# A hybrid encoder layer on one core: where two additions, eight bank drains and the row factor are done

## The chip, the cores and the metric

The kernel runs on one core of a Trainium2 chip. The metric is device time in microseconds (us) of one execution, the median over several runs. TensorE (PE in the profile) does matrix products into PSUM; VectorE (DVE), ScalarE (ACT) and GpSimd (POOL) do elementwise work; SyncE (SP) issues the loads. Every engine works its own queue in order, and they meet only by semaphores.

## What is computed

One layer over 256 tokens of width 2048, batch 1, all in float32. The input is normalised by row, multiplied by `w_in`, and its columns go to three mixers (attention in a neighbourhood, an RWKV7 recurrence in both directions, retention); their outputs are concatenated and multiplied by `w_out`; a feed-forward part with `w_up` and `w_down` (8192 wide) follows. The parts that matter here:

```python
h = rms_norm(x, pre_mix_g[l]);  z = h @ w_in[l]          # row factor 1/rms, one for each token
# attention: softmax(q k^T * 64**-0.5 + bias) v, 8 heads of 64
# recurrence, end: y = layer_norm(y) * lnx_g + lnx_b ; y = y + bonus ; y_rw = y * g
# retention, 6 heads of 128:
q = rotary_interleaved(q, ang); k = rotary_interleaved(k, ang) * d ** -0.5
#   rotary: stack([x0 * cos - x1 * sin, x0 * sin + x1 * cos])
o = intra + cross; o = o * rsqrt(mean(o * o) + eps); yc = o * silu(g)
y = concatenate([ya, yb, yc]) @ w_out[l]
```

## The kernel before

**Weights.** All weight matrices stream through as halves of 128x1024 values. SP loads a half into `raw` (four slots). ScalarE rounds it to float32r, `hi` (L1614, `w_hi`), VectorE forms the rest, `lo` (L979, `w_lo`), three slots each. TensorE multiplies high by high, high by low and low by high (L2065, L2066, L2071 and others). This stream goes on for the whole kernel.

**Groups.** `w_in` gives 57 tiles of 128 columns, in 29 groups of two. The first 11 groups belong to the recurrence. Of the other 18, two tiles fill one PSUM bank (6 or 7 in turn) as 128x512. Groups 11 and 12 are the attention's queries, 13 and 14 its keys, 15 and 16 its values, 17 and 18 the first values of retention, 19 to 24 the pairs (query, key) of retention heads 0 to 5, 25 more values, 26 to 28 the gates. Values are drained by ScalarE with a factor per token (`by_token`). The other 13 groups are drained by VectorE: `scaled_nr` (L1016, its instruction L1023) multiplies the bank by `row_scale`, the row factor, on its way to SBUF, and raises `bank_free`. Draining group g waits for `bank_free` of the group before, and TensorE starts group g when g-2 is drained.

**Gaps.** The products of `w_in` are cut into "gaps" by a list of depths, `DONE`. Every engine has its own `gap()`, in which it does its share of what is due by then: drains of groups first, then `hi` or `lo`. Between gaps an engine does the mixers' work, written out by hand. `stage_a` runs the recurrence (six tiles, its last a tail of four chunks); the mix stage follows.

**Mix stage.** It has six turns, `turn(i)` on each engine, one for each retention head; the first four also carry two attention heads each. In turn i:
- GpSimd, ahead of it, turns head i by the table: L913 multiplies query and key by `cos` into `qk_cos`, L917 the key's halves by `sin` into `qk`. L917 waits for `st_done`, the retention scores of head i-1 (L2481 on TensorE).
- VectorE, in `rotate(i)`: L1394 multiplies the query's halves by `sin`, L1398 adds `qk_cos`. L1398 waits for `rot_in`, all four products of GpSimd.
- VectorE: `scale_q(i)` (L1353, four instructions, reading the query's tokens backwards, times 64**-0.5) feeds the attention scores; `maxima(i)` adds the bias (L1369) and takes negative maxima (L1374, L1377). ScalarE exponentiates (L1901, `weights`). VectorE divides by the sums (`scale_p`: L1403, L1405). TensorE transposes the result (`turn_p`, L2471), ScalarE copies it back (L1866).
- In turn 0 VectorE also does, behind `maxima(1)`, `summed_recurrence` (L1381, `y_rw` plus the bonus in `zr`, 128x1536) and `gated_recurrence` (L1386, times `gate`), which raises `y_rw_ready`. ScalarE waits for `y_rw_ready` before it writes `o_all` (L1933), which lies over `gate`.

GpSimd's work ahead of the mix stage is the attention bias: it waits for `table_in` (the table with `win`, `cos`, `sin`) and `bias_in`, and adds `win` to eight heads (L905).

## Time and profile before

| | |
|---|---|
| median of three runs | 1303.27 us (1302.81 to 1303.52) |
| the profiled execution | 1303.43 us, span in the trace 1301.6 us |
| granted TensorE clock, mean | 0.998 of full speed |
| busy: PE, DVE, ACT, POOL | 1284.9, 825.2, 644.9, 323.6 us |
| chain that ended last | PE 91%, DVE 4%, all others 1% or less |

The span is the time from the first to the last instruction in the trace; the profiled execution took 1.83 us more than it. Times within the trace, such as 434.92, count from the start of the span. An idle stretch of an engine stands in square brackets behind the instruction that ended it, with the releaser. Rows of one engine overlap by a few tens of ns where the next instruction is already under way.

### The profile page before, as it was taken

What the parts mean: (1) busy time and instruction counts of PE and PEld (TensorE: products, weight loads), DVE (VectorE), ACT (ScalarE), POOL (GpSimd) and SP (SyncE); (2) the same over time, 40 slices, a digit from 0 to 9 for tenths busy, and PEclk for the clock granted to TensorE, in tenths of its full rate; (3) what the DMA queues carried; (4) which work ended last, traced back from release to release, by engine and by line L of the source; (5) the groups of instructions that cost most, each with busy time, mean ns of one, the idle gap of its engine ahead of it and who ended that gap; (6) DMA issues with size and microseconds to landing.
All of it is one profiled execution on the core that took longest, in us unless ns stands there. A gap on an engine that the chain in (4) does not pass through costs nothing.

```text
span 1301.6 us, 24350 instructions
## 1 busy us (share of the span) xinstructions
PE 1284.9 (99%) x9986; PEld 1103.2 (85%) x9986; DVE 825.2 (63%) x1148; ACT 644.9 (50%) x985; POOL 323.6 (25%) x266
## 2 busy tenths in 40 slices
PE   9999999999999999999999999999999999999997
PEld 7888888778899898888888888888888888888886
DVE  7778887887767877556555555555555555555564
ACT  6565655555435565546444444444444444444453
POOL 0224332333214320002444445555510000000000
PEclk9999999999999999999999999999999999999999
DMA  9766333342385456745766666666655555555572
GB/s 302 196 180 191 100 87 108 88 115 82 113 187 162 116 154 224 259 146 150 224 194 186 188 192 189 186 192 190 189 191 194 192 193 194 194 194 193 194 239 86
DMA packets 267695, 226.24 MB, mean 174 GB/s; under 512 B 15232, under 2 KB 240640, under 8 KB 266944
## 3 DMA queue, kind: packets, MB, share of 16 engines
q1 hardware_dynamic: 267344, 223.51, 57.0%
q8 instruction: 79, 1.29, 0.4%
q0 software_dynamic: 240, 1.18, 0.3%
q14 instruction: 32, 0.26, 0.1%
HBM read 222.56 MB, written 2.10 MB: 173 GB/s over the span
## 4 chain that ended last, share of the span: by engine, by line
PE 91%; DVE 4%; SPq 1%; DMA 1%; issue 1%; ACT 1%; DVEq 0%; ACTq 0%
PE psum L2535 33%; PE psum L2081 23%; PE psum L2092 12%; PE psum L2065 3%; PE psum L2071 3%; PE psum L2066 3%; PE psum L2145 2%; PE psum L2308 1%; DVE w_lo L979 1%; PE psum L2147 1%; PE psum L2152 1%; SPq L743 1%; PE psum L2243 1%; PE psum L2106 1%; PE psum L2323 1%
## 5 line engine op out<-in xcount | busy, mean ns | idle before, releaser
L979 DVE TENSOR_TENSOR w_lo<-raw,w_hi 128x1024 fp32r<-128x1024 f32 x393 | 500.9, 1277 | 373.8 <-ACT w_hi L1614 370.8
L1614 ACT ACTIVATE w_hi<-raw 128x1024 fp32r<-128x1024 f32 x393 | 417.7, 1064 | 440.6 <-PE psum L2535 196.9
L2535 PE MATMUL psum<-w_hi,act_both 128*128 128x512 f32 x1216 | 327.6, 389 | 0.1
L2081 PE MATMUL psum<-act_both,w_hi 128*128 128x512 f32 x1296 | 315.4, 392 | 0.0
L2081 PEld LDWEIGHTS psum<-act_both,w_hi 128*128 128x128 f32 x1296 | 237.0, 188 | 45.2 <-issue 0.2
L2535 PEld LDWEIGHTS psum<-w_hi,act_both 128*128 128x128 f32 x1216 | 228.0, 188 | 48.6 <-DVE arena L1555 0.5
L2535 PE MATMUL psum<-w_lo,act_both 128*128 128x512 f32 x608 | 187.5, 389 | 0.0
L2092 PEld LDWEIGHTS psum<-act_both,w_lo 128*128 128x128 f32 x1296 | 169.4, 191 | 7.7
L2092 PE MATMUL psum<-act_both,w_lo 128*128 128x256 f32 x1296 | 173.2, 283 | 0.0
L2535 PEld LDWEIGHTS psum<-w_lo,act_both 128*128 128x128 f32 x608 | 114.1, 188 | 23.6
L924 POOL TENSOR_TENSOR arena<-arena 128x512 f32<-128x512 f32 x32 | 42.3, 1323 | 285.8 <-DVE arena L1555 285.8
L2065 PE MATMUL psum<-act_both,w_hi 128*128 128x256 f32 x416 | 113.1, 304 | 0.0
L2066 PE MATMUL psum<-act_both,w_hi 128*128 128x256 f32 x416 | 104.2, 282 | 0.0
L2065 PEld LDWEIGHTS psum<-act_both,w_hi 128*128 128x128 f32 x416 | 78.8, 189 | 5.3 <-issue 1.2
L2066 PEld LDWEIGHTS psum<-act_both,w_hi 128*128 128x128 f32 x416 | 79.2, 190 | 0.2
L927 POOL TENSOR_SCALAR arena<-arena 128x512 f32<-128x512 f32 x32 | 74.1, 2314 | 2.8
L2071 PE MATMUL psum<-act_both,w_lo 128*128 128x256 f32 x416 | 68.8, 283 | 0.7 <-DVE w_lo L979 0.7
L929 POOL TENSOR_TENSOR arena<-arena 128x512 f32<-128x512 f32 x32 | 61.5, 1922 | 2.7
L2071 PEld LDWEIGHTS psum<-act_both,w_lo 128*128 128x128 f32 x416 | 58.0, 191 | 1.3 <-DVE w_lo L979 1.3
L2145 PE MATMUL psum<-w_hi,act_both 128*128 128x512 f32 (+1 forms) x96 | 37.2, 396 | 0.2 <-DVE arena L1023 0.2
L826 POOL TENSOR_TENSOR arena<-arena,row_scale 128x512 f32<-128x512 f32 (+1 forms) x11 | 18.1, 1649 | 68.6 <-DVE arena L1014 46.2
L2147 PE MATMUL psum<-w_hi,act_both 128*128 128x512 f32 (+1 forms) x96 | 33.4, 357 | 0.0
(251 smaller groups left out, 1238.0 us busy)
## 6 DMA issues: line engine op xcount, KB each, us to landing
raw<-in_w_up SPq DMA_DIRECT2D x128, 512.0 KB, 4.0
raw<-in_w_down SPq DMA_DIRECT2D x128, 512.0 KB, 4.4
raw<-in_w_in SPq DMA_DIRECT2D x113, 512.0 KB, 4.1
raw<-in_w_out SPq DMA_DIRECT2D x32, 512.0 KB, 4.7
arena<-in_na_rpb SPq DMA_DIRECT2D x16, 128.0 KB, 5.2
arena<-in_x SPq DMA_DIRECT2D x2, 1024.0 KB, 7.2
arena<-in_x_t SPq DMA_DIRECT2D x3, 512.0 KB, 7.7
out_x<-arena SPq DMA_DIRECT2D x3, 512.0 KB, 2.7
```

The lines of the kernel that those rows point to most:

```text
L927: pool.tensor_scalar(r, r, 0.0, None, ALU.max).then_inc(s["up_scaled"], 1)
L929: pool.tensor_tensor(u[:, 2 * q:2 * q + 2], r, r, ALU.mult).then_inc(s["relu_free"], 1)
L979: dve.tensor_tensor(by_half(h, low(h)), by_pair(h, raw[:, place[h] % RAW]), by_half(h, high(h)).bitcast(F32), ALU.subtract).then_inc(s["lo ...
L1614: act.activation(by_half(h, high(h)), by_pair(h, raw[:, place[h] % RAW]), ACT.Copy).then_inc(s["hi_half"], 1)
L2065: pe.matmul(dst, w_hi[:, h % SPLIT, at:at + P], act_hi[:, kt], start=kt == 0, stop=False)
L2066: pe.matmul(dst, w_hi[:, h % SPLIT, at:at + P], act_lo[:, kt], start=False, stop=False)
L2071: last = pe.matmul(dst, w_lo[:, h % SPLIT, at:at + P], act_hi[:, kt], start=False, stop=kt == KT - 1)
L2081: last = pe.matmul(bank[b], w_hi[:, h % SPLIT, at:at + P], act_both[:, kt].rearrange("p a t -> p (a t)"), start=kt == 0, stop=stop and kt ...
L2092: last = pe.matmul(bank[b][:, 0:T], w_lo[:, h % SPLIT, at:at + P], act_hi[:, kt], start=False, stop=stop and kt == kts[-1])
L2145: pe.matmul(dst, act_lo[:, kt, tokens], w, start=kt == 0 and (t == 0 or count == 4), stop=False, skip_group_check=count != 4)
L2147: pe.matmul(dst, act_hi[:, kt, tokens], w, start=False, stop=False, skip_group_check=count != 4)
L2535: last = pe.matmul(bank[4 * t + 2 * j + b], lhs[:, tokens], w[:, b * 512:(b + 1) * 512], start=start, stop=stop)
```

## The change

- `summed_recurrence` and `gated_recurrence` leave VectorE's turn 0. GpSimd does both, between its rotations of head 1 and of head 2, and waits for their end before it goes on.
- GpSimd multiplies `cos` and `sin` in the table by `row_scale` once (one 128x512 operation), ahead of the bias. VectorE's first rotation waits for that (`table_scaled`) in place of `table_in`.
- `scale_q` multiplies by 64**-0.5 and by `row_scale` in one instruction of the other form.
- With the factor in the table and in the queries, eight groups need none at the drain: 11 and 12 (attention queries) and 19 to 24 (retention queries and keys). ScalarE copies their banks (`copy_nr`) where VectorE multiplied them. Groups 13, 14, 26, 27 and 28 stay with VectorE.

```diff
+        def plain(g):
+            j = 2 * (g - RW_GROUPS)
+            return 0 <= j < NA_T // 3 or PLACE_OF[RET_Q(0)] <= j <= PLACE_OF[RET_K(RET_CT - 1)]
 # gpsimd
             pool.wait_ge(s["table_in"], 16)
+            angles = table[:, LATE["cos"][0]:LATE["sin"][1]].rearrange("p (a t) -> p a t", a=2)
+            pool.tensor_tensor(angles, angles, row_scale.unsqueeze(1).broadcast_to([P, 2, T]), ALU.mult).then_inc(
+                s["table_scaled"], 1)
+            pool.wait_ge(s["table_scaled"], 1)
...
+            def summed_recurrence():
+                pool.wait_ge(s["yt_taken"], RW_CT)
+                pool.tensor_tensor(y_rw, y_rw, zr, ALU.add).then_inc(s["y_rw_sum"], 1)
+            def gated_recurrence():
+                pool.wait_ge(s["y_rw_sum"], 1)
+                pool.wait_ge(s["gate_ready"], 3)
+                pool.tensor_tensor(y_rw, y_rw, gate, ALU.mult).then_inc(s["y_rw_ready"], 1)
...
+                if i == 1:
+                    pool.wait_ge(s["rot_in"], 4 * i + 4)
+                    summed_recurrence()
+                    gated_recurrence()
+                    pool.wait_ge(s["y_rw_ready"], 1)
 # vector
-                    if wide_of(at["nr"]) is None:
+                    if wide_of(at["nr"]) is None and not plain(at["nr"]):
                         scaled_nr(at["nr"])
...
-                    last = dve.tensor_scalar(q_s[:, h * GRID_W:(h + 1) * GRID_W], backwards(na_q(i), h * GRID_W),
-                                             NA_HD ** -0.5, None, ALU.mult)
+                    last = dve.scalar_tensor_tensor(q_s[:, h * GRID_W:(h + 1) * GRID_W], backwards(na_q(i), h * GRID_W),
+                                                    NA_HD ** -0.5, backwards(row_scale, h * GRID_W), ALU.mult, ALU.mult)
...
-                if i == 0:
-                    summed_recurrence()
-                    gated_recurrence()
 # scalar
+            def copy_nr(g):
+                tiles = group_tiles(g)
+                j = tiles[0] - RW_T
+                act.wait_ge(s["gemm_half"], 2 * (tiles[-1] + 1))
+                act.wait_ge(s["bank_free"], g)
+                place_free(act, j)
+                act.activation(cut(nr_at(j), 2 * T), bank[6 + g % 2], ACT.Copy).then_inc(s["bank_free"], 1)
...
                     if wide_of(at["wide"]) is not None:
                         by_token(at["wide"])
+                    elif plain(at["wide"]):
+                        copy_nr(at["wide"])
```

How the queues stand. Line numbers of the changed kernel differ; operands name the arrays they lie in, `arena` for nearly all.

GpSimd, from the bias to the rotation of head 2, before (L913 and L917 are a rotation):

```order
L905 TENSOR_TENSOR arena<-arena,arena_later 128x512 x8
L913 TENSOR_TENSOR arena_later<-arena,arena_later 128x256 x2
L917 TENSOR_TENSOR arena_later<-arena,arena_later 64x256 x2
L913 TENSOR_TENSOR arena_later<-arena,arena_later 128x256 x2
L917 TENSOR_TENSOR arena_later<-arena,arena_later 64x256 x2
L913 TENSOR_TENSOR arena_later<-arena,arena_later 128x256 x2
```

and changed (L931 and L935 are a rotation, L907 the table, L920 and L925 sum and gate):

```order
L907 TENSOR_TENSOR arena_later<-arena_later,row_scale 128x512
L914 TENSOR_TENSOR arena<-arena,arena_later 128x512 x8
L931 TENSOR_TENSOR arena_later<-arena,arena_later 128x256 x2
L935 TENSOR_TENSOR arena_later<-arena,arena_later 64x256 x2
L931 TENSOR_TENSOR arena_later<-arena,arena_later 128x256 x2
L935 TENSOR_TENSOR arena_later<-arena,arena_later 64x256 x2
L920 TENSOR_TENSOR arena_later<-arena_later,arena 128x1536
L925 TENSOR_TENSOR arena_later<-arena_later,arena 128x1536
L931 TENSOR_TENSOR arena_later<-arena,arena_later 128x256 x2
```

The table stands ahead of all of it, and two operations on 128x1536 between the second and the third rotation.

VectorE, from the end of `rotate(1)` in turn 0 to the first `scale_p` of turn 1, before:

```order
L1398 TENSOR_TENSOR arena_later<-arena_later 128x512
L1023 TENSOR_TENSOR arena<-psum,row_scale 128x512
L979 TENSOR_TENSOR w_lo<-raw,w_hi 128x1024
L1369 TENSOR_TENSOR arena_later<-psum,arena 128x1024
L1374 TENSOR_REDUCE small<-arena_later 128x4
L1377 TENSOR_SCALAR small<-small 128x4
L1381 TENSOR_TENSOR arena_later<-arena_later,arena 128x1536
L1386 TENSOR_TENSOR arena_later<-arena_later,arena 128x1536
L1403 RECIPROCAL small<-small 128x2
L1405 TENSOR_TENSOR arena_later<-arena_later,small 128x512
```

and changed:

```order
L1412 TENSOR_TENSOR arena_later<-arena_later 128x512
L1002 TENSOR_TENSOR w_lo<-raw,w_hi 128x1024
L1392 TENSOR_TENSOR arena_later<-psum,arena 128x1024
L1397 TENSOR_REDUCE small<-arena_later 128x4
L1400 TENSOR_SCALAR small<-small 128x4
L1417 RECIPROCAL small<-small 128x2
L1419 TENSOR_TENSOR arena_later<-arena_later,small 128x512
```

Three operations are gone between the rotation and `scale_p`: the drain of group 24, the sum and the gate.

ScalarE, in the recurrence's last chunk, where group 22 is due (L1843 and L1865 take a gate bank, L1817 and L1839 one product of the chunk, L1821 and L1843 of the changed kernel the next, L1614 and L1625 are `hi`), before:

```order
L1843 ACTIVATE arena<-psum 128x512
L1817 ACTIVATE arena<-psum 128x128
L1614 ACTIVATE w_hi<-raw 128x1024
L1821 ACTIVATE arena_later<-psum 64x2x64
L1614 ACTIVATE w_hi<-raw 128x1024 x3
```

and changed:

```order
L1865 ACTIVATE arena<-psum 128x512
L1839 ACTIVATE arena<-psum 128x128
L1668 ACTIVATE arena<-psum 128x512
L1625 ACTIVATE w_hi<-raw 128x1024
L1843 ACTIVATE arena_later<-psum 64x2x64
L1625 ACTIVATE w_hi<-raw 128x1024 x3
```

The copy stands right ahead of a `hi`; the seven others do too.

## Rows read from the trace of the kernel before

**Rows 1.** Page: the span, and the engines' busy time, share and instructions.

```profile
span 1301.6 us, 24350 instructions
...
PE 1284.9 (99%) x9986; PEld 1103.2 (85%) x9986; DVE 825.2 (63%) x1148; ACT 644.9 (50%) x985; POOL 323.6 (25%) x266
```

**Rows 2.** TensorE's waits: line, releaser, us in total, times, longest.

```profile
PE psum L2471 <- DVE arena_later L1405: 1.7, 1, 1.7
```

**Rows 3.** Timeline of VectorE, 422 to 435: start, length, line, operation, [idle before].

```profile
422.40 1.22 DVE L979 TENSOR_TENSOR w_lo<-raw,w_hi 128x1024 fp32r<-128x1024 f32 x1 [1.72 <-ACT w_hi L1614]
...
425.15 0.68 DVE L1023 TENSOR_TENSOR arena<-psum,row_scale 128x512 f32<-128x512 f32 x1
425.75 1.44 DVE L979 TENSOR_TENSOR w_lo<-raw,w_hi 128x1024 fp32r<-128x1024 f32 x1
...
429.60 0.17 DVE L1377 TENSOR_SCALAR small<-small 128x4 f32<-128x4 f32 x1
429.68 1.75 DVE L1381 TENSOR_TENSOR arena_later<-arena_later,arena 128x1536 f32<-128x1536 f32 x1
431.47 2.18 DVE L1386 TENSOR_TENSOR arena_later<-arena_later,arena 128x1536 f32<-128x1536 f32 x1
...
433.75 1.02 DVE L1405 TENSOR_TENSOR arena_later<-arena_later,small 128x512 f32<-128x512 f32 x1
```

**Rows 4.** Timeline of TensorE, at 434.9.

```profile
434.92 0.41 PE L2471 MATMUL psum<-cst,arena_later 128*128 128x128 f32 x2 [1.68 <-DVE arena_later L1405]
```

**Rows 5.** Timeline of ScalarE, at 422.9 and 429.8.

```profile
422.85 1.06 ACT L1614 ACTIVATE w_hi<-raw 128x1024 fp32r<-128x1024 f32 x1 [0.49 <-PE psum L2071]
429.81 0.51 ACT L1901 ACTIVATE arena_later<-arena_later,small 128x256 f32<-128x256 f32 x1 [5.89 <-DVE small L1377]
```

**Rows 6.** Timeline of GpSimd, 386 to 435.

```profile
386.45 11.94 POOL L905 TENSOR_TENSOR arena<-arena,arena_later 128x512 f32<-128x512 f32 x8 [3.82 <-DMA arena_later<-in_late]
...
411.31 1.44 POOL L913 TENSOR_TENSOR arena_later<-arena,arena_later 128x256 f32<-128x256 f32 x2 [8.00 <-DVE arena_later L1398]
414.61 1.88 POOL L917 TENSOR_TENSOR arena_later<-arena,arena_later 64x256 f32<-64x256 f32 x2 [1.86 <-PE psum L2481]
425.37 2.41 POOL L913 TENSOR_TENSOR arena_later<-arena,arena_later 128x256 f32<-128x256 f32 x2 [8.88 <-DVE arena_later L1398]
430.82 3.41 POOL L917 TENSOR_TENSOR arena_later<-arena,arena_later 64x256 f32<-64x256 f32 x2 [3.04 <-PE psum L2481]
```

**Rows 7.** Timeline of VectorE one turn later, 441 to 448.

```profile
441.73 0.85 DVE L1394 TENSOR_TENSOR arena_later<-arena,arena_later 64x256 f32<-64x256 f32 x2
...
445.74 0.17 DVE L1377 TENSOR_SCALAR small<-small 128x4 f32<-128x4 f32 x1
...
447.27 0.69 DVE L1405 TENSOR_TENSOR arena_later<-arena_later,small 128x512 f32<-128x512 f32 x1
```

**Rows 8.** Single lines: count, shortest/median/longest ns, first and last start.

```profile
L905 POOL TENSOR_TENSOR arena<-arena,arena_later x8: 1286/1302/2308, 386.4 to 396.1; 128x512 f32<-128x512 f32 x8
...
L913 POOL TENSOR_TENSOR arena_later<-arena,arena_later x12: 728/739/1724, 398.3 to 473.7; 128x256 f32<-128x256 f32 x12
...
L979 DVE TENSOR_TENSOR w_lo<-raw,w_hi x393: 1205/1226/2172, 10.2 to 1275.4; 128x1024 fp32r<-128x1024 f32 x197
...
L1353 DVE TENSOR_SCALAR arena_later<-arena x16: 177/181/725, 402.6 to 451.5; 128x64 f32<-128x64 f32 x16
```

**Rows 9.** ScalarE's groups by shape, 300 to 500: busy us, mean ns.

```profile
L1866 ACT ACTIVATE arena_later<-psum 128x512 f32<-128x512 f32 x8 | 4.8, 598 | 11.8 <-PE psum L2471 11.8
```

**Rows 10.** Timelines at 396: VectorE, then TensorE.

```profile
395.65 0.29 DVE L1279 COPY arena_later<-psum 64x128 f32<-64x128 f32 x1
...
396.09 0.30 PE L2413 MATMUL psum<-arena_later 128*64 128x64 f32 x3 [0.21 <-DVE arena_later L1279]
```

**Rows 11.** Timelines at 180: ScalarE, then TensorE.

```profile
179.76 0.29 ACT L1817 ACTIVATE arena<-psum 128x128 f32<-128x128 f32 x1
...
180.55 0.25 PE L2387 MATMUL psum<-arena 64*64 64x64 f32 x2
```

More of the change, by code:

```diff
@@ L436, in layer @@
         s = {n: sem(n) for n in (
-            "consts_in", "vec_in", "lora_in", "g2_in", "bias_in", "table_in", "decay_in", "gain_in", "x_again", "out_written",
+            "consts_in", "vec_in", "lora_in", "g2_in", "bias_in", "table_in", "table_scaled", "decay_in", "gain_in", "x_again", "out_written",
             "eps_set", "ones_set", "first_x_in", "first_raw_in", "first_hi", "first_lo", "x_squared", "x_added", "x_totalled", "x_summed", "row_root", "row_ready", "token_root", "token_ready", "token_done", "xt_done", "h_hi", "h_lo",
@@ L1377, in maxima @@
                 dve.tensor_scalar(top, top, -1.0, None, ALU.mult).then_inc(s["mx_ready"], 1)
-            def summed_recurrence():
-                dve.wait_ge(s["yt_taken"], RW_CT)
-                dve.tensor_tensor(y_rw, y_rw, zr, ALU.add).then_inc(s["y_rw_sum"], 1)
-            def gated_recurrence():
-                dve.wait_ge(s["y_rw_sum"], 1)
-                dve.wait_ge(s["gate_ready"], 3)
-                dve.tensor_tensor(y_rw, y_rw, gate, ALU.mult).then_inc(s["y_rw_ready"], 1)
             def rotate(i):
@@ L1390, in rotate @@
                 if i == 0:
-                    dve.wait_ge(s["table_in"], 16)
+                    dve.wait_ge(s["table_scaled"], 1)
                 dve.wait_ge(s["st_done"], i)
```

## The prediction

> **What bounds the kernel now.** I read the page first. TensorE is busy 1284.9 of 1301.6 us [rows 1], so the most that any change of the other engines can give back is what TensorE idles, 16.7 us, and the start and the end of the kernel hold a good part of that. A busy share of 63% on VectorE or 25% on GpSimd says nothing here. The second view is therefore TensorE's waits, one by one. Where a wait names an operation that the change touches, or one queued behind it, the change can pay. The longest of these is the transpose of the softmax in turn 1 (L2471), which waits 1.7 us for VectorE's L1405 [rows 2]. Then come the timelines around it.
>
> On TensorE the transpose starts at 434.92 after 1.68 us idle, so TensorE was ready at 433.24 [rows 4]. On VectorE the maxima end at 429.77 (429.60 + 0.17). Then the sum (429.68, 1.75 us) and the gate (431.47, 2.18 us) run to 433.65, and only then L1405, at 433.75 for 1.02 us, to 434.77 [rows 3]. ScalarE began the exponentials at 429.81 [rows 5], so they were not what was late. The 3.9 us of sum and gate stand in VectorE's queue in front of the one thing that TensorE wants.
>
> **Sum and gate leave VectorE.** What is late next? One turn later the same step has nothing between: from the end of the maxima (445.74 + 0.17 = 445.91) to the end of the first L1405 (447.27 + 0.69 = 447.96) it takes 2.05 us [rows 7]. In turn 1 the maxima also come 0.68 us earlier, since the drain of group 24 (425.15) leaves VectorE too [rows 3]: 429.77 - 0.68 = 429.09, and L1405 ends at 431.14. TensorE asks at 433.24. Cover 2.1 us, so the whole 1.68 us goes. Afterwards TensorE, VectorE and ScalarE are all 1.68 us earlier; their steps wait for each other and for TensorE, and the DMA has landed long before, so nothing takes it back that I can find.
>
> **The same two on GpSimd.** It can begin when the rotation of head 1 is done: L917 at 414.61 for 1.88, so 416.49 [rows 6]. The trace has no 128x1536 operation on GpSimd. Bounds: 128x512 takes 1.302 us and 128x256 takes 0.739 [rows 8], 0.563 us for 256 columns more, so 1536 columns take 1.302 + 4 x 0.563 = 3.55 us and both 7.1 us: done at 423.6. The upper bound is the worst stretch in the rows, 1724 against 728 ns for L913 [rows 8], 2.37 times: 16.8 us, done at 433.3. VectorE works half of this stretch on operands in SBUF, and a mixed stretch is L905's, eight in 11.94 us where 8 x 1.302 is 10.4 [rows 6, 8]; a bad one is the L917 pair at 430.82, 3.41 against 1.88 us [rows 6]. I take 1.4 times, 10 us: done at 426.5.
>
> Who waits? Queued behind them on GpSimd is the rotation of head 2. L913 began at 425.37 and took 2.41 us, then waited 3.04 us for TensorE's L2481, until 430.82 [rows 6]. At 426.5 it ends at 428.9, well ahead of that. Even from 433.3 the pairs of 2.41 and 3.41 us would end at 439.1, and VectorE's part of that rotation began at 441.73 [rows 7], now about 440.0. The other reader is ScalarE's `o_all`, held by `y_rw_ready`; that came at 433.65 before, and would now come at 426.5, at the worst bound at 433.3. Both are covered: price 0.
>
> The price on VectorE is contention. Gate against sum, same shape, is 2.18 against 1.75 us while L917 ran beside it [rows 3, 6]; L979 goes from 1.205 to 2.172 us at the worst [rows 8]. Behind 422.40, where VectorE still idles 1.72 us for ScalarE [rows 3], two L979 and a rotation can meet GpSimd's two operations: 0 to 2 x 0.97 + 0.5 = 2.4 us. Of the 2.1 us cover that leaves +2.1 to -0.3 us: at the worst 0.3 us of the wait stays. I take about 1 us of stretch and no price.
>
> The Trainium skill speaks against this part: GPSIMD Engine Reference, Key points, says that GpSimd shares its SBUF interfaces with VectorE, with contention from VectorE instructions that read two SBUF inputs, and that VectorE is about twice as fast at elementwise work. The trace agrees in direction (3.55 us worked out against 1.75 us measured). By that rule the two cost more engine time than they save; it would change the sum only if the cover of 2.1 us were used up.
>
> **The table by the row factor.** One more 128x512 operation on GpSimd at 386.45, 1.3 to 2.3 us by L905's range [rows 8]. It pushes the bias and the rotation of head 0 back by as much. After that rotation GpSimd idled 8.00 us for VectorE's L1398 [rows 6]: it was far ahead. Price 0; without that cover it would be 1.3 to 2.3 us.
>
> **The query scaling.** Sixteen L1353 of 0.181 us [rows 8] become the two-input form. Between no change and the length of one under contention, 0.725 us; near the lower end, since 64 columns are mostly fixed cost. I take +0.05 us each, 0.2 us a turn. In each turn VectorE next waits for a `hi`, or the scores it feeds are asked for later. Price 0.
>
> **Eight drains change engine.** VectorE gives back 8 x 0.68 us. ScalarE takes a plain PSUM copy of 128x512 each, 0.598 us (L1866) [rows 9], 4.8 us in all. Each stands right ahead of a `hi` that waits for the same progress of TensorE, so it never waits for more than that `hi` did; it delays it by 0.6 us. Two places matter.
> - Group 22, at 394. VectorE's L1279 began at 395.65, behind the drain, and TensorE waited 0.21 us for it until 396.09 [rows 10]. Without the drain L1279 comes 0.6 us earlier. ScalarE's half of the same value (L1821) comes 0.6 us later, behind its copy. Gain 0.2 us; 0 if L1821 is then late in turn.
> - Group 12, at 176. ScalarE's copy comes ahead of the L1817 that ended at 180.05, and TensorE used it at 180.55 [rows 11]. A slack of 0.5 us against 0.6 us: loss 0.1 us, at most 0.6.
>
> At group 24, `hi` ran at 422.85 [rows 5]; copied first it ends at 424.5, and VectorE wants it at 425.15. The other copies fall into idle time of ScalarE.
>
> **The sum.** -1.68 - 0.2 + 0.1 = -1.8 us. The profiled execution took 1303.43 us, 0.16 over the median 1303.27; the median becomes 1301.5 us, 0.14% less. A measurement of this kernel can tell about 0.2%, 2.6 us, from no change, so I call this "same".
>
> **Rivals.**
> - Contention eats the cover. L1405 in turn 1 is still late by up to 1.7 us, because both engines stretch each other (the rule of the skill, carried to its end). For it: 2.37 times for L913 and 1.8 times for L979. Against it: the cover of 2.1 us and the idle 1.72 us at 422.40. Time 1302 to 1303.3. Chance 0.12.
> - The 1.7 us is only moved: TensorE comes earlier to the next `lo` or `hi`, which was just in time, and waits there. For it: VectorE is busy nearly without a break in turns 0 to 3. Against it: those steps are themselves released by TensorE. Time about 1303. Chance 0.09.
> - More goes than I count: TensorE's short stalls for VectorE in the recurrence and the mix stage, too short to be listed or listed at well under 1 us, shrink as VectorE loses 8 x 0.68 + 3.9 = 9.3 us. Against it: only the drain at 394 stands ahead of such a wait. Some 2 us more, 1299.5 us. Chance 0.10.
> - Slower: `hi` is in fact what TensorE's next half hangs on, and the eight copies push it. 8 x 0.6 = 4.8 us, less 1.9: 1303.27 + 2.9 = 1306.2 us. It decides where the slack of a `hi` is under 0.6 us. Against it: in the whole list of TensorE's waits `w_hi` is named once, at the kernel's start. Chance 0.07.
>
> **How the numbers follow.** The forecast, 1300.8 to 1302.3, has 0.62. The two cases where the gain fails (0.21) end within 0.2% too. Faster by over 0.2%: 0.10. Slower: 0.07. Within: 0.83. The range reaches down towards the third rival and up over the first two, and leaves the slow one out: 1300.2 to 1303.6.
>
> **What would show it.** Right: no wait of TensorE before the transpose of turn 1, VectorE going from maxima straight to `scale_p`; sum and gate on GpSimd from about 415 to 427, 4 to 6 us each, with the rotation of head 2 behind them still waiting for TensorE; no wait before the state product at 396; copies on ScalarE of 0.6 us; TensorE's busy time unchanged. Wrong: a wait for L1405 or for a `lo` in turn 1 or 2; ScalarE's `o_all` waiting for GpSimd; TensorE waiting for `w_hi`; a new wait of over 0.3 us near group 12 or 19; a change of the span outside 390 to 440.

## The result, and the profile after

The changed kernel takes 1310.43 us (median of six, 1309.70 to 1311.43), the kernel before 1303.30 us beside it (median of six, 1302.81 to 1303.88). The ratio is 1.0055, with a 95% interval of 1.0045 to 1.0066: **slower by 7.1 us**, where 1301.5 us was predicted and 1303.6 us was the upper end.

The page has the span, and the engines' busy time, share and instructions, against [rows 1]:

```profile
span 1308.8 us, 24353 instructions
...
PE 1287.5 (98%) x9986; PEld 1104.9 (84%) x9986; DVE 825.5 (63%) x1138; ACT 648.1 (50%) x993; POOL 330.9 (25%) x269
```

TensorE has as many instructions as before and is busy 2.6 us more; VectorE has ten instructions fewer and is busy no less (825.5 against 825.2 us). Both are signs: something made the same work slower.

TensorE's waits come next (line, releaser, us in total, times, longest). The 1.7 us for the softmax scaling [rows 2] are gone, as forecast. In their place:

```profile
PE psum L2093 <- DVE w_lo L1002: 6.1, 3, 5.4
...
PE psum L2409 <- ACT arena L1839: 1.2, 1, 1.2
...
PE psum L2400 <- issue: 0.7, 1, 0.7
...
PE psum L2480 <- ACT arena_later L1878: 0.2, 1, 0.2
```

The first row's 5.4 us is one wait for a low half, `w_lo`, of which nothing in the change speaks. VectorE's timeline there (start, length, line, operation) says why it was late:

```profile
418.13 3.81 DVE L1419 TENSOR_TENSOR arena_later<-arena_later,small 128x512 f32<-128x512 f32 x1
421.86 4.43 DVE L1002 TENSOR_TENSOR w_lo<-raw,w_hi 128x1024 fp32r<-128x1024 f32 x1
...
427.43 1.21 DVE L1002 TENSOR_TENSOR w_lo<-raw,w_hi 128x1024 fp32r<-128x1024 f32 x1
```

L1419 is the scaling of the softmax, `scale_p`, of turn 0; it takes 3.81 us, where the same shape took 0.69 us [rows 7]. L1002 is the subtraction that makes the low half; it takes 4.43 us, against 1.2 us in the last row and in [rows 8]. Neither had to wait for a semaphore; the lost time is inside the instructions. GpSimd's timeline has what ran beside them, the table (L907), the rotation (L935, L931), the sum (L920) and the gate (L925):

```profile
388.70 1.27 POOL L907 TENSOR_TENSOR arena_later<-arena_later,row_scale 128x512 f32<-128x512 f32 x1 [5.40 <-DMA arena_later<-in_late]
...
415.93 1.54 POOL L935 TENSOR_TENSOR arena_later<-arena,arena_later 64x256 f32<-64x256 f32 x2 [1.20 <-PE psum L2503]
417.55 3.84 POOL L920 TENSOR_TENSOR arena_later<-arena_later,arena 128x1536 f32<-128x1536 f32 x1
421.47 3.75 POOL L925 TENSOR_TENSOR arena_later<-arena_later,arena 128x1536 f32<-128x1536 f32 x1
433.47 1.73 POOL L931 TENSOR_TENSOR arena_later<-arena,arena_later 128x256 f32<-128x256 f32 x1 [8.26 <-DVE arena_later L1412]
```

Put side by side, the ends answer each other. The sum ends at 421.39 (417.55 + 3.84), and the scaling that began at 418.13 ends at 421.94, 0.55 us later. The gate ends at 425.22, and the low half that began at 421.86 ends at 426.29, 1.07 us later. Each VectorE instruction did nearly all of its own work (0.69 and 1.22 us) after the GpSimd instruction had ended. By this it was not slowed down but **held**; the experiments below test that.

The trace of the kernel before has the same picture in small. Here is one of its two longest L979 [rows 8], with the GpSimd product beside it:

```profile
91.34 2.17 DVE L979 TENSOR_TENSOR w_lo<-raw,w_hi 128x1024 fp32r<-128x1024 f32 x1 [0.26 <-ACT w_hi L1614]
```

```profile
91.23 1.20 POOL L826 TENSOR_TENSOR arena<-arena,row_scale 128x512 f32<-128x512 f32 x1 [9.58 <-DVE arena L1014]
```

The product ends at 92.43 and L979 1.08 us later, at 93.51.

TensorE's timeline behind the wait (the low products, the transposes of the softmax, the scores of head pair 1):

```profile
426.35 1.65 PE L2093 MATMUL psum<-act_both,w_lo 128*128 128x256 f32 x6 [5.42 <-DVE w_lo L1002]
427.80 1.05 PE L2493 MATMUL psum<-cst,arena_later 128*128 128x128 f32 x4
428.79 2.08 PE L2480 MATMUL psum<-arena,arena_later 64*128 64x256 f32 x8
```

and the busy time of the engines and the granted TensorE clock in stretches of 5 us (the clock is the last but two):

```profile
415.00:420.00 5.00, 5.00 (x41) 4.89 (x41) 3.73 (x6) 3.95 (x11) 3.92 (x3) 1.00 0.04 13
420.00:425.00 5.00, 0.94 (x8) 0.73 (x7) 5.00 (x2) 0.73 (x1) 4.92 (x2) 0.89 0.00 0
425.00:430.00 5.00, 3.65 (x16) 3.15 (x18) 3.63 (x8) 1.10 (x2) 0.21 (x1) 0.50 0.42 110
430.00:435.00 5.00, 5.00 (x39) 3.69 (x36) 4.37 (x6) 1.98 (x3) 1.53 (x1) 0.92 0.71 203
```

Behind the wait the granted clock is 0.50 of full speed, the lower of the two levels, 1.2 instead of 2.4 GHz. Until 420 it stood at 1.00; then TensorE did nothing for 5.4 us. The six low products take 1.65 us.

One smaller loss stands earlier. ScalarE's timeline at 333 us, first after, then before (L1668 is the copy of group 19, L1625 and L1614 the high half behind it):

```profile
332.83 0.59 ACT L1668 ACTIVATE arena<-psum 128x512 f32<-128x512 f32 x1
333.45 1.14 ACT L1625 ACTIVATE w_hi<-raw 128x1024 fp32r<-128x1024 f32 x1
```

```profile
333.02 1.17 ACT L1614 ACTIVATE w_hi<-raw 128x1024 fp32r<-128x1024 f32 x1
```

and what TensorE does with it at 341 us, after and before:

```profile
341.19 0.45 PE L2400 MATMUL psum<-arena 64*64 64x64 f32 x8 [0.74 <-issue]
```

```profile
340.52 0.45 PE L2378 MATMUL psum<-arena 64*64 64x64 f32 x8 [0.20 <-issue]
```

The copy puts the high half 0.43 us later, the low half and the recurrence's chain on VectorE follow, and TensorE waits 0.74 instead of 0.20 us.

### The profile page after: what moved, and what is told of

Same layout as the page of the kernel before. It is cut to its first block, busy times and chain, and to the rows that moved or that the text cites. A ratio compares the mean times of both kernels' runs of the same rounds, so it can differ in the third digit from the quotient of the medians.

```text
span 1308.8 us, 24353 instructions
## 1 busy us (share of the span) xinstructions
PE 1287.5 (98%) x9986; PEld 1104.9 (84%) x9986; DVE 825.5 (63%) x1138; ACT 648.1 (50%) x993; POOL 330.9 (25%) x269
## 4 chain that ended last, share of the span: by engine, by line
PE 68%; DVE 3%; issue 1%; SPq 1%; ACT 1%; DMA 1%; DVEq 0%; POOL 0%; ACTq 0%
PE psum L2557 33%; PE psum L2103 18%; PE psum L2114 9%; PE psum L2087 1%; PE psum L2093 1%; PE psum L2088 1%; SPq L748 1%; DVE w_lo L1002 1%; DMA raw<-in_w_in 1%; PE psum L2534 0%; PE psum L2480 0%; PE psum L2167 0%; PE psum L2174 0%; PE psum L2169 0%; PE psum L2493 0%
## 5 line engine op out<-in xcount | busy, mean ns | idle before, releaser
L1002 DVE TENSOR_TENSOR w_lo<-raw,w_hi 128x1024 fp32r<-128x1024 f32 x393 | 505.5, 1288 | 378.2 <-ACT w_hi L1625 374.3
L1625 ACT ACTIVATE w_hi<-raw 128x1024 fp32r<-128x1024 f32 x393 | 417.7, 1064 | 439.1 <-PE psum L2557 195.7
```

What stands on the lines that cost most here:

```text
L1002: dve.tensor_tensor(by_half(h, low(h)), by_pair(h, raw[:, place[h] % RAW]), by_half(h, high(h)).bitcast(F32), ALU.subtract).then_inc(s["lo ...
L1625: act.activation(by_half(h, high(h)), by_pair(h, raw[:, place[h] % RAW]), ACT.Copy).then_inc(s["hi_half"], 1)
```

## The experiments

Two theories were to be told apart from the start. By the first, a VectorE instruction that meets a GpSimd instruction is held until that one ends, so the price goes by the length of one instruction. By the second, the two engines share a rate, so the price goes by the amount of work. Beside them stood two questions: what the clock costs, and what the other three parts of the change do. Every run has the time of the kernel before on the same chip beside it: 1302.71 us in the first series of four, 1302.69 in the second, 1302.61 in the third.

### The rest of the change alone

The changed kernel; the two calls leave GpSimd's loop and stand in VectorE's `turn` again:

```
-                if i == 1:
-                    pool.wait_ge(s["rot_in"], 4 * i + 4)
-                    summed_recurrence()
-                    gated_recurrence()
-                    pool.wait_ge(s["y_rw_ready"], 1)
...
                     maxima(i + 1)
+                if i == 0:
+                    summed_recurrence()
+                    gated_recurrence()
```

> The changed kernel with the sum and the gate back on VectorE, where they stood: the scaled angle table, the query scaling and the eight ScalarE copies alone. Theory (the long GpSimd instructions are what costs): the 5.4 us wait of the low products is not there, the 1.7 us wait for the softmax scaling is there again, the granted clock stays at 1.00 in 400 to 450 us, and the time is 1303.3 to 1304.6 us, the part above 1303.3 being the ScalarE copies' own price (the low halves ran 0.3 to 1.0 us late between 345 and 402 us in the changed kernel). Rival (the copies and the table carry a good part of the loss): 1306 us or more.

Measured: 1301.64 us, ratio 0.9993 (0.9984 to 1.0002), so 1.1 us under before, and below the range that I had set, though the interval takes in 1. The 5.4 us wait is gone and the clock stays at 1.00. TensorE's timeline shows the transposes of turn 1:

```profile
433.23 0.63 PE L2491 MATMUL psum<-cst,arena_later 128*128 128x128 f32 x4 [0.47 <-DVE arena_later L1414]
```

The wait there is 0.47 us, not the 1.68 of [rows 4]. I had expected it back in full. It is shorter because group 24's bank is no longer emptied by VectorE ahead of it, the 0.68 us that the prediction worked out; and the two operations took 1.75 and 1.76 us in this execution, against 1.75 and 2.18 [rows 3]. So the other parts do not carry the loss.

### The move alone

The kernel before, with the two operations defined and called on GpSimd, behind the rotation of head 1:

```
-                if i == 0:
-                    summed_recurrence()
-                    gated_recurrence()
...
+                if i == 1:
+                    pool.wait_ge(s["rot_in"], 4 * i + 4)
+                    summed_recurrence()
+                    gated_recurrence()
+                    pool.wait_ge(s["y_rw_ready"], 1)
```

> The kernel before with the sum and the gate moved to GpSimd and nothing else changed. Theory (the long GpSimd instructions are what costs): one VectorE instruction near 418 us takes some 3.8 us instead of 0.7 to 0.9 and the low half behind it some 4.4 instead of 1.2, TensorE waits 5 to 6 us for it, the clock falls behind it, and the time is 1308 to 1310 us. Rival (the parts only hurt together): under 1305 us.

Measured: 1308.33 us, ratio 1.0039 (1.0024 to 1.0054), 5.6 us over before. VectorE's timeline and TensorE's wait:

```profile
416.26 3.79 DVE L1410 TENSOR_TENSOR arena_later<-arena_later,small 128x512 f32<-128x512 f32 x1
419.98 4.43 DVE L993 TENSOR_TENSOR w_lo<-raw,w_hi 128x1024 fp32r<-128x1024 f32 x1
```

```profile
PE psum L2073 <- DVE w_lo L993: 6.1, 3, 5.4
```

The same two instructions are held for the same lengths, 3.79 and 4.43 us, and TensorE waits the same 5.4 us. The move does it by itself.

### The changed kernel once more

Unchanged, in the second series, since the two runs above add up to 4.5 us and not to 7.1.

> The changed kernel once more, unchanged, beside the others of this series. The move alone cost 5.6 us and the rest alone gained 1.1 us, 4.5 us together, where the whole change lost 7.1 us. If the parts hinder each other (the copies make the low halves late, and the long GpSimd instructions then hit a VectorE without slack), this run is again 6.5 to 7.5 us above before. If 7.1 us was partly a matter of when transfers landed in those executions (a raw half landed 1.3 us later at 393 us in its trace), it is 4 to 6 us above before, and the 2.3 us that stood between the two traces at 415 us are not there.

Measured: 1309.00 us, ratio 1.0051 (1.0035 to 1.0066), 6.3 us over before: between the two cases that I had set, within reach of both. Its waits:

```profile
PE psum L2093 <- DVE w_lo L1002: 6.1, 3, 5.4
...
PE psum L2400 <- issue: 0.8, 1, 0.8
```

The 1.2 us of L2409 above, at 395 us (0.5 us before, behind a half that landed 1.3 us earlier), are not among them, and the scaling of turn 0 starts at 416.04, where it starts at 416.11 before and at 418.13 in the first profile of the changed kernel. So that wait belongs to that one execution, and I do not count it as the change's. The wait at 341 us (L2400) is there in both.

That settles the sum of the parts, 5.6 - 1.1 against 6.3. Alone, the rest shortens the wait of turn 1 from 1.68 to 0.47 us and adds 0.55 us at 341 us: 0.7 us by the trace, of the 1.1 measured (its interval reaches from 2.1 us less to 0.3 more). Beside the move that wait is gone already, there is nothing to shorten, and only the cost is left: 5.6 + 0.55 = 6.2.

### The same work in twelve pieces

The sum, and the gate in the same way, in steps of one tile of 256 columns:

```
-                pool.tensor_tensor(y_rw, y_rw, zr, ALU.add).then_inc(s["y_rw_sum"], 1)
+                for n in range(0, RW_CT, 1):
+                    last = pool.tensor_tensor(y_rw[:, n:n + 1], y_rw[:, n:n + 1], zr[:, n:n + 1], ALU.add)
+                last.then_inc(s["y_rw_sum"], 1)
```

The expectation:

> The changed kernel with the sum and the gate each cut into six GpSimd instructions of 128x256 in the same place, the same elements in all. Theory (a VectorE instruction is held until the GpSimd instruction that runs beside it ends): a GpSimd piece takes 0.6 to 0.8 us, no VectorE instruction between 417 and 427 us takes more than 0.9 us over its own time, the low half of 421.9 us ends by 424, TensorE waits under 2.5 us for it instead of 5.4, and the time is 1302.5 to 1306 us. Rival (the two engines share a rate, and the same elements cost the same however they are cut): the two VectorE instructions together still lose over 5 us, TensorE waits 4.5 us or more, and the time stays within 1308.5 to 1311 us.

Measured: 1303.70 us, ratio 1.0007 (0.9998 to 1.0016). With the same elements on the same engine in the same place, that is 5.3 us less than the changed kernel of the second series (1309.00). VectorE's timeline (L1006 the low half, L1380 the query scaling), GpSimd's two lines (count, shortest/median/longest ns), and TensorE's wait:

```profile
416.97 1.76 DVE L1006 TENSOR_TENSOR w_lo<-raw,w_hi 128x1024 fp32r<-128x1024 f32 x1
...
419.31 2.27 DVE L1380 SCALAR_TENSOR_TENSOR arena_later<-arena,row_scale 128x64 f32<-128x64 f32 x4
```

```profile
L921 POOL TENSOR_TENSOR arena_later<-arena_later,arena x6: 718/900/1709, 415.4 to 420.6; 128x256 f32<-128x256 f32 x6
...
L928 POOL TENSOR_TENSOR arena_later<-arena_later,arena x6: 727/1044/1724, 421.5 to 427.2; 128x256 f32<-128x256 f32 x6
```

```profile
421.74 1.14 PE L2484 MATMUL psum<-arena,arena_later 64*128 64x256 f32 x8 [1.54 <-DVE arena_later L1380]
```

The low half takes 1.76 instead of 4.43 us, and the scaling ahead of it 1.04 instead of 3.80: together they lose 0.9 us, where the rate theory had asked for over 5. It falls by its own condition. Over the kernel with both operations on VectorE (1301.64 us) the long pair costs 7.4 us and the twelve pieces 2.1. But the pieces are not free. They stand back to back, so nearly every VectorE instruction meets one, and from 416.0 to 429.5 us VectorE's instructions lose some 5.3 us in all against that kernel, not much less than the 6.3 us of the two holds. What changed is where it falls: most of it lies behind the low half that TensorE waited for. It shows in one place: the four small products of the query scaling take 2.27 us together, where 0.61 us is usual, and TensorE waits 1.54 us for them. And the holding goes both ways: a piece takes 0.72 us at the shortest and 1.72 at the longest, where I had expected 0.6 to 0.8, and the twelve together 12.9 us, against 7.6 for the two long ones.

### One long instruction instead of two

The changed kernel with the sum alone on GpSimd, behind the rotation of head 1, and the gate alone in VectorE's `turn`:

```
+                if i == 1:
+                    pool.wait_ge(s["rot_in"], 4 * i + 4)
+                    pool.wait_ge(s["yt_taken"], RW_CT)
+                    pool.tensor_tensor(y_rw, y_rw, zr, ALU.add).then_inc(s["y_rw_sum"], 1)
+                    pool.wait_ge(s["y_rw_sum"], 1)
...
+                if i == 0:
+                    gated_recurrence()
```

> The changed kernel with the sum alone on GpSimd, in the place of the change, and the gate back on VectorE in its old place: one long GpSimd instruction instead of two. Theory (each VectorE instruction is held to the end of the GpSimd instruction beside it): one instruction of VectorE (the softmax scaling near 416 to 418 us) takes 3.8 us, the low half behind it its own 1.2 us, the low products wait 2.2 to 3 us instead of 5.4, the later 1.7 us wait is gone or under 0.8, and the time is 1303 to 1306.5 us. Rival (a fixed cost for using GpSimd there, whatever the length): 1308 us or more.

Measured: 1305.01 us, ratio 1.0016 (1.0007 to 1.0025). VectorE, GpSimd, TensorE:

```profile
416.59 3.80 DVE L1415 TENSOR_TENSOR arena_later<-arena_later,small 128x512 f32<-128x512 f32 x1
420.31 1.21 DVE L993 TENSOR_TENSOR w_lo<-raw,w_hi 128x1024 fp32r<-128x1024 f32 x1
```

```profile
416.01 3.83 POOL L930 TENSOR_TENSOR arena_later<-arena_later,arena 128x1536 f32<-128x1536 f32 x1
```

```profile
421.58 0.98 PE L2091 MATMUL psum<-act_both,w_lo 128*128 128x256 f32 x6 [2.19 <-DVE w_lo L993]
```

One instruction is held (3.80 us), the next has its own time again (1.21 us), and TensorE waits 2.19 us. This is the run that gives the law its numbers. In the changed kernel TensorE went idle at 426.35 - 5.42 = 420.93. Without holds the scaling (0.69 us from 418.13) and the low half behind it (1.22 us) would have been done at about 419.97: a slack of 0.96 us. One hold of 3.11 us less 0.96 is 2.15, measured 2.19. Two holds, 3.12 + 3.21 = 6.33, less 0.96 is 5.37, measured 5.42.

The median holds more than that wait. 2.19 of new wait, 1.68 gone and 0.55 at 341 us make 1.1 us, and 2.3 were measured. TensorE's attention scores right behind the wait point to the clock:

```profile
422.93 1.91 PE L2478 MATMUL psum<-arena,arena_later 64*128 64x256 f32 x8
```

The same eight take 1.13 us at the full clock (next run), and the granted clock here is 0.81 from 420 to 425 us and 0.84 from 425 to 430. That the clock accounts for all of the rest is my estimate; no run filled this wait.

### The clock alone

The half with the late low part is half 97. Ahead of its low products:

```
+                if h == 97 and kts[0] % HALF_KT == 0:
+                    for _ in range(42):
+                        pe.matmul(bank[1][:, T:2 * T], w_hi[:, h % SPLIT, 0:P], act_hi[:, 0], start=True, stop=True)
                 if kts[0] % HALF_KT == 0:
                     pe.wait_ge(s["lo_half"], h + 1)
```

> The changed kernel with 42 matmuls of 128x256 on operands that are there already, into half a bank that nothing reads, put in front of the low products that wait 5.4 us: TensorE works through the wait. They take some 0.12 us each, 5.0 us in all, no more than the wait. Theory (the fall of the granted clock behind the wait costs some 3 us of the 7): the granted clock stays at 1.00 from 420 to 435 us, and the time is 1307 to 1308 us. Rival (the low clock costs nothing, since the work behind it waits for VectorE and ScalarE anyway): 1310 to 1311 us.

Measured: 1306.95 us, ratio 1.0031 (1.0019 to 1.0042), 2.05 us under the unchanged kernel of the next series, with nearly the same time of before in both (1302.71, 1302.69). TensorE's timeline, the filling first:

```profile
418.46 5.20 PE L2091 MATMUL psum<-act_both,w_hi 128*128 128x256 f32 x42
424.13 0.98 PE L2096 MATMUL psum<-act_both,w_lo 128*128 128x256 f32 x6 [0.47 <-DVE w_lo L1002]
424.94 0.60 PE L2496 MATMUL psum<-cst,arena_later 128*128 128x128 f32 x4
425.47 1.13 PE L2483 MATMUL psum<-arena,arena_later 64*128 64x256 f32 x8
```

The wait is 0.47 us instead of 5.42, and TensorE still does nothing useful until 424.13 (424.25 in the unchanged kernel of the second series); but the clock stays at 1.00 throughout. The three groups behind it take 0.98, 0.60 and 1.13 us, where they took 1.65, 1.05 and 2.08 above: 2.07 us of difference, and 2.05 in the median. So a third of the loss is not the wait but what it did to the clock. I had expected 3 us, and 1307 us at the least.

### Which VectorE instructions are held

The sum on VectorE, placed earlier (see the next run), and the gate on GpSimd inside the rotation of head 2:

```
                     pool.tensor_tensor(qk_cos[:, n], src, late_const("cos"), ALU.mult).then_inc(s["rot_in"], 1)
+                if i == 2:
+                    pool.wait_ge(s["rot_in"], 4 * i + 2)
+                    pool.wait_ge(s["y_rw_sum"], 1)
+                    pool.wait_ge(s["gate_ready"], 3)
+                    pool.tensor_tensor(y_rw, y_rw, gate, ALU.mult).then_inc(s["y_rw_ready"], 1)
+                    pool.wait_ge(s["y_rw_ready"], 1)
```

> As the run with the sum ahead on VectorE, and the gate on GpSimd behind the first two products of head 2's rotation, near 427 to 431 us, beside VectorE's sum with the scores (one operand in PSUM), its maxima (one operand) and a product of four elements a row. Theory (only a VectorE instruction with two operands in SBUF is held): GpSimd's gate takes 3.7 to 3.9 us, the reduction beside it stays at 1.22 us, the softmax scaling behind it is held under 1.5 us, and the time is within 1.5 us of the run with the sum ahead. Rival (every VectorE instruction is held beside a GpSimd instruction): the reduction or the sum with the scores takes 3 us or more, and TensorE waits over 2 us for what follows.

Measured: 1302.34 us, ratio 0.9998 (0.9989 to 1.0007). VectorE's timeline (sum of scores and bias, maxima, product of 4 elements a row by -1) and GpSimd's gate:

```profile
425.91 1.22 DVE L1384 TENSOR_TENSOR arena_later<-psum,arena 128x1024 f32<-128x1024 f32 x1
427.16 1.22 DVE L1389 TENSOR_REDUCE small<-arena_later 128x4 f32<-128x1024 f32 x1
428.41 2.46 DVE L1392 TENSOR_SCALAR small<-small 128x4 f32<-128x4 f32 x1
```

```profile
427.35 3.48 POOL L927 TENSOR_TENSOR arena_later<-arena_later,arena 128x1536 f32<-128x1536 f32 x1
```

The product of four elements a row, 0.17 us elsewhere, takes 2.46 us: it starts at 428.41 and ends at 430.87, when the gate does (427.35 + 3.48 = 430.83). It has one operand, so my theory of two operands was too narrow: `tensor_scalar` is held too. The maxima (one operand, 128x1024) run from 427.16 to 428.38, the gate from 427.35: they overlap for a microsecond, the maxima take their usual 1.22 us, and the gate is 0.3 us shorter than in the changed kernel, so neither held the other. The sum of scores and bias, with one operand in PSUM, takes its 1.22 us beside GpSimd's first two products of that rotation (425.00 to 427.28). Behind a long GpSimd instruction that had started ahead of it neither kind was seen; behind short ones both were, and neither was held. In the changed kernel the maxima of turn 0 start at 414.31, inside the second product of L931 (413.28 to 414.72 for the two), and take 1.22 us. In the run with twelve pieces the two products out of PSUM behind the low half start at 418.65, inside a piece that runs from 417.61 to 419.32, and take their usual 0.74 us.

The Trainium skill, SBUF — State Buffer, section Who interferes with whom, states this pattern: VectorE and GpSimd share one pair of ports under an exclusive lock, and whichever comes second is blocked, not throttled; a VectorE instruction with two SBUF inputs contends with a GpSimd instruction that reads SBUF, `tensor_scalar` can contend in a two-port mode, and `tensor_reduce` on this chip never does. This case's rows agree (3.81, 4.43 and 2.46 us held; 1.22, 1.22 and 0.74 us not). In which mode the product of four elements ran, no trace here shows, nor the ports themselves.

### The sum ahead, within VectorE's own order

```
                 if attend:
                     gap()
+                    if i == 0:
+                        summed_recurrence()
                     gap()
...
                 if i == 0:
-                    summed_recurrence()
                     gated_recurrence()
```

> The kernel with the rest of the change alone (sum and gate on VectorE), and the sum moved ahead within VectorE's own order, between the two gaps of turn 0, where VectorE stood idle for 1.72 us waiting for a high half of 422.4 us. The sum takes 1.75 us. Theory: it fills that idle time, the low half of 422.4 us starts at most 0.2 us later, the softmax scaling of turn 1 is ready 1.7 us earlier, TensorE's wait of 1.68 us for it is gone and nothing takes its place: 1300.0 to 1301.2 us, 1.5 to 3 us under before. Rival (the sum delays the low half that TensorE needs next): 1302 us or more.

Measured: 1301.33 us, ratio 0.9989 (0.9980 to 0.9997), 1.4 us under before. A little less gain than the 1.5 us I had set as the least. VectorE's timeline:

```profile
419.56 1.22 DVE L988 TENSOR_TENSOR w_lo<-raw,w_hi 128x1024 fp32r<-128x1024 f32 x1
420.70 1.75 DVE L1390 TENSOR_TENSOR arena_later<-arena_later,arena 128x1536 f32<-128x1536 f32 x1
422.37 1.22 DVE L988 TENSOR_TENSOR w_lo<-raw,w_hi 128x1024 fp32r<-128x1024 f32 x1
```

The sum stands where VectorE idled 1.72 us in [rows 3]; the low half behind it starts at 422.37, where it started at 422.40. There is no wait at the transposes of turn 1 in TensorE's list.

The same edit on the kernel before, with nothing of the change:

> The kernel before with one edit: the sum of the recurrence, on VectorE as ever, moved ahead within its order, between the two gaps of turn 0. Theory (the 1.68 us wait was an ordering matter within VectorE alone, and the table, the query scaling and the copies add nothing measurable): TensorE's wait of 1.68 us is gone or under 0.3, and the time is 1.0 to 1.9 us under before, 0.9985 to 0.9993 of it. Rival (the gain of the run with the sum ahead and the rest of the change, 1.36 us, came from the rest of the change): within 0.5 us of before.

Measured: 1300.96 us, ratio 0.9987 (0.9978 to 0.9996), 1.6 us under before, as much as the wait of 1.68 us that went. VectorE again:

```profile
420.03 1.75 DVE L1381 TENSOR_TENSOR arena_later<-arena_later,arena 128x1536 f32<-128x1536 f32 x1
421.84 1.23 DVE L979 TENSOR_TENSOR w_lo<-raw,w_hi 128x1024 fp32r<-128x1024 f32 x1
```

### Groups 12 and 19 back on VectorE

The kernel with the sum ahead and the rest of the change, with these two groups copied by VectorE (plain, without the factor):

```
+                    elif at["nr"] in (12, 19):
+                        plain_nr(at["nr"])
...
+                dve.tensor_copy(cut(nr_at(j), 2 * T), bank[6 + g % 2]).then_inc(s["bank_free"], 1)
...
-                    elif plain(at["wide"]):
+                    elif plain(at["wide"]) and at["wide"] not in (12, 19):
                         copy_nr(at["wide"])
```

> The run with the sum ahead and the rest of the change, with the copies of groups 12 and 19 back on VectorE as plain copies out of PSUM (the factor stays in the table and the query scaling). Theory (the copy of group 19 ahead of a high half on ScalarE is what makes the 0.7 to 0.8 us wait near 341 us, of which 0.2 was there before): that wait is 0.2 us again, and the time is 0.3 to 0.7 us under the run with the sum ahead. Rival (the wait has another cause): the wait stays at 0.7 us or more and the time is the same within 0.3 us.

Measured: 1300.42 us, ratio 0.9982 (0.9973 to 0.9990), 2.2 us under before. ScalarE at 332 us and TensorE at 340 us:

```profile
332.33 1.15 ACT L1635 ACTIVATE w_hi<-raw 128x1024 fp32r<-128x1024 f32 x1
```

```profile
339.85 0.45 PE L2410 MATMUL psum<-arena 64*64 64x64 f32 x8 [0.23 <-issue]
```

The high half follows at once, and the wait is 0.23 us. So the copy of group 19 was the cause of the longer wait. This is the fastest kernel of the study, and it beats both the kernel before and the changed one. Against the two runs with the sum ahead (0.9989, 0.9987) the intervals overlap. Its median lies 0.9 us under the first of them, more than the 0.3 to 0.7 that I had set, and the trace accounts for 0.5: that it is faster rests on those 0.5 us, not on the medians.

## Why the prediction was wrong, point by point

**The step that failed** is the price of contention: "Behind 422.40 ... two L979 and a rotation can meet GpSimd's two operations: 0 to 2 x 0.97 + 0.5 = 2.4 us", and from it "I take about 1 us of stretch and no price". Two things were wrong in it.
- The size. The 0.97 us was the longest stretch of L979, beside a GpSimd product of 1.20 us (91.23 above). I read it as a rate, or as a worst case of the engine, and it followed the length of its neighbour. Beside two operations that the prediction itself put at 3.55 us each, the bound from the same rows should have been near 3.5 us for each VectorE instruction met. Measured: 3.12 and 3.21 us, together 6.3.
- The place. The prediction starts GpSimd at 416.49 and counts VectorE's instructions only from 422.40, because it looked at the wait that was to go. Between the two stand the scaling of turn 0 and the low half behind it. They were in no list of waits, since they had 0.96 us of slack, and that was all the cover there was. The start was off too: in the second series the sum began at 415.46, ahead of the scaling at 416.04, where the prediction has 416.49, behind a scaling that began at 416.11 before.

**What it set off.** 6.33 - 0.96 = 5.4 us of wait, and 2.1 us by the clock, which no step of the prediction had (it forecast TensorE's busy time unchanged; that rose by 2.6 us). With the 1.7 us that went and 0.5 us from group 19: 5.4 + 2.1 - 1.7 + 0.5 = 6.3 us, the difference measured in the second series. The first comparison had 7.1; the 0.8 us between them I leave open, and the half that landed late at 393 us may be part of it.

**Sum and gate leave VectorE:** right. The wait at the transposes of turn 1 is gone in every run with the move. But the two runs with the sum ahead get the same 1.7 us for one moved line, and pay nothing.

**The same two on GpSimd:** the duration came near the lower bound (3.84 + 3.75 = 7.6 us, where 7.1 was the bound and 10 was taken; 417.55 to 425.22, 416.5 to 426.5 forecast). Who waits on GpSimd's side was right too: the rotation of head 2 (L931, 433.47) begins after 8.26 us idle, and `o_all` never waited.

**The rule that was weighed** (the Trainium skill, GPSIMD Engine Reference, Key points) was taken for a matter of engine time and of the 2.1 us of cover at turn 1. It says that there is contention and not how it goes; the Trainium skill, SBUF — State Buffer, section Who interferes with whom, says how. By the prediction's own 3.55 us for each operation, two holds would have come to 7.1 us at most, less the slack of 0.96: an estimate of up to 6.1 us of wait, where 5.4 were measured.

**The table:** right, 1.27 us at 388.70 and no wait from it. **The query scaling:** right by itself, 0.211 us a product against 0.181 [rows 8]; in twelve pieces' company it was what TensorE waited for.

**Eight drains:** the wait of [rows 10] is gone, as forecast for group 22, but it is also missing in the run with the move alone, where VectorE still drains that group; so the 0.2 us are not shown to be its gain. At group 12 [rows 11] no wait is listed. "The other copies fall into idle time of ScalarE" was wrong for group 19, which cost 0.55 us; "a new wait of over 0.3 us near group 12 or 19" was on the list of what would show it wrong, and did. The 0.2 us of L2480 above stand behind the copy of group 23, but the second profile of the changed kernel does not list them; I leave them open.

**The rivals.** "Contention eats the cover" had the mechanism and, like the forecast, the wrong size: it ended at 1303.3 because it counted at most the gain as lost. "Slower" had the other mechanism, `hi` pushed by copies, which is real at one of eight places (0.55 us of the 4.8 counted). None of the four let the moved work reach a half that TensorE had not been waiting for.

## What to carry to other kernels

- Before moving work to GpSimd, take the length of its longest single instruction, and lay it beside every VectorE instruction that needs two operands out of SBUF, or is a `tensor_scalar` on SBUF, from the moment GpSimd can start, not from the wait that is to be removed. Each one met can end that much later; subtract the slack of its reader. Short pieces bound the hold, but back to back they hold nearly everything.
- A bound taken from a trace holds for the conditions of that row. The longest stretch of an instruction beside short neighbours is no bound for long ones.
- If an operation is late only because it stands in a queue behind others, look for an idle stretch of the same engine first. Here one moved line was worth 1.6 us, and the move to another engine cost 6.

## What the runs showed of the hardware

- A hold appears inside the instruction's own duration (4.43 us for 1.22 us of work), so VectorE's busy time counts it as work: 825.5 us with ten instructions fewer.
- Even a tiny instruction is held: four elements a row, 0.17 us alone, 2.46 us beside the gate.
- Holding goes both ways: GpSimd's pieces of 0.72 us took up to 1.72 us.
- One wait of 5.4 us cost TensorE 2.1 us more behind it, at a granted clock of 0.50. The wait of 2.19 us had clocks of 0.81 and 0.84 in the two stretches of 5 us around and behind it.
